# Turning attention probabilities: a product with diag(1/sum) against normalization on VectorE and a turn by the identity

## The reference

```
logits = einsum('bthd,btkhd->bthk', q, k_sel) * A_HEAD_DIM ** -0.5
logits = where(valid, logits, -inf)
p = softmax(logits, axis=-1)
return einsum('bthk,btkhd->bthd', p, v_sel)
```

## Time and profile before

| | |
|---|---|
| median of 3 runs | 1298.71 us (1297.08 to 1299.79) |
| profiled execution, its own time | 1302.94 us |
| its span, first to last instruction | 1301.3 us |
| TensorE busy (matmuls) | 1123.8 us, 86% |
| VectorE busy | 624.9 us, 48% |
| ScalarE busy | 321.8 us, 25% |
| mean granted TensorE clock | 0.93 |

### The profile page before, as it was taken

How to read it: one execution, slowest core, us unless ns; L and a number is a source line. 1 busy time by engine, 2 the same in 40 slices (tenths; PEclk the granted TensorE clock), 3 DMA queues, 4 the chain that set the end, 5 groups by cost and what they waited for, 6 DMA issues and landing times.

```text
span 1301.3 us, 24857 instructions
## 1 busy us (share of the span) xinstructions
PE 1123.8 (86%) x9930; PEld 682.8 (52%) x9930; DVE 624.9 (48%) x1363; ACT 321.8 (25%) x758; POOL 162.9 (13%) x225
## 2 busy tenths in 40 slices
PE   8999999997899279998599999999789973999930
PEld 3577778973545223332256777899454541333310
DVE  0056899867243511111643589988653443011128
ACT  0243341305321111111244343322242210211100
POOL 0140008005000110000301000350410002000030
PEclk9999999998899589999799999999989975999975
DMA  7199110008450869996522111100486057699742
GB/s 293 45 391 379 51 64 18 7 13 283 184 225 9 348 234 377 420 423 240 191 77 60 64 49 65 33 22 5 147 293 239 24 214 279 254 418 425 290 153 89
DMA packets 58357, 240.56 MB, mean 185 GB/s; under 512 B 8738, under 2 KB 20162, under 8 KB 48834
## 3 DMA queue, kind: packets, MB, share of 16 engines
q1 hardware_dynamic: 38608, 169.15, 33.8%
q0 software_dynamic: 14592, 52.10, 10.9%
q10 hardware_dynamic: 5042, 17.71, 3.4%
HBM read 190.38 MB, written 50.78 MB: 185 GB/s over the span
## 4 chain that ended last, share of the span: by engine, by line
PE 83%; DVE 6%; ACT 3%; issue 3%; DMA 2%; DVEq 2%; POOL 1%; POOLq 0%; ACTq 0%
PE ps L767 20%; PE ps L1360 13%; PE ps L936 11%; PE ps L1317 9%; PE ps L1375 7%; PE ps L747 4%; PE ps L713 4%; PE ps L1185 2%; PE ps L1347 2%; ACT arena L1452 1%; PE ps L827 1%; PE ps L723 1%; PE ps L1284 1%; PE ps L1296 1%; DVEq L2545 1%
## 5 line engine op out<-in xcount | busy, mean ns | idle before, releaser
L1452 ACT ACTIVATE arena<-ps 128x512 f32<-128x512 f32 (+11 forms) x336 | 140.3, 454 | 599.2 <-PE ps L767 148.3
L767 PE MATMUL ps<-arena 128*128 128x272 f32 x1088 | 259.7, 396 | 0.0
L767 PEld LDWEIGHTS ps<-arena 128*128 128x128 f32 x1088 | 204.9, 190 | 48.8 <-issue 4.9
L1360 PE MATMUL ps<-arena 128*32 128x512 f32 x1536 | 169.7, 592 | 4.8 <-ACT arena L1452 4.8
L936 PE MATMUL ps<-arena 64*64 64x64 f32 (+3 forms) x4016 | 145.2, 231 | 3.9 <-DVE arena L2248 2.5
L936 PEld LDWEIGHTS ps<-arena 64*64 64x64 f32 x4016 | 134.6, 134 | 15.0 <-issue 10.0
L1317 PE MATMUL ps<-arena 128*128 128x512 f32 x256 | 115.8, 609 | 0.0
L1360 PEld LDWEIGHTS ps<-arena 128*32 128x32 f32 x1536 | 51.3, 109 | 116.9 <-issue 116.9
L1375 PE MATMUL ps<-arena 128*32 128x512 f32 x768 | 87.4, 595 | 3.4 <-DVE arena L2713 2.0
L1317 PEld LDWEIGHTS ps<-arena 128*128 128x128 f32 x256 | 48.6, 194 | 58.9 <-issue 58.8
L2707 DVE COPY arena<-ps 128x256 f32<-128x256 f32 x24 | 10.2, 425 | 140.2 <-PE ps L1392 140.2
(11 more groups left out here) (351 smaller groups left out, 1287.8 us busy)
## 6 DMA issues: line engine op xcount, KB each, us to landing
arena<-in_w_gu SPq DMA_DIRECT2D x32, 2048.0 KB, 13.7
arena<-in_w_dn SPq DMA_DIRECT2D x32, 1024.0 KB, 14.4
arena<-in_wf SPq DMA_DIRECT2D x34, 512.0 KB, 3.7
rows_in<-arena POOLq DMA_DIRECT2D x12, 1024.0 KB, 25.8
arena<-rows_in SPq DMA_DIRECT2D x24, 512.0 KB, 13.7
rows_out<-arena ACTq DMA_DIRECT2D x24, 512.0 KB, 8.6
arena<-in_cache_v POOLq DMA_DIRECT2D x64, 128.0 KB, 5.6
arena<-in_cache_k SPq DMA_DIRECT2D x64, 128.0 KB, 6.8
```

The lines of the kernel that those rows point to most:

```text
L767: mm = pe.matmul(ps[:, 2 + 2 * h + n % 2, 0:HALF], m.wf[n % 3][:, c, :], m.xT[:, c, h * HALF:h * HALF + HALF], start=c == 0, stop=c == KC - 1)
L1360: mm = pe.matmul(ps[q, 3 + k, :], m.xgT[:, c, q], m.w_gu[HOME[i]][:, c, :], start=c == 0, stop=c == KC - 1, skip_group_check=True)
L1452: return act.activation(out, in_, ACT.Copy)
```

## The change

VectorE no longer multiplies the tile of probabilities. It multiplies the identity, for each of the four heads, with the reciprocal sums of the rows, which gives four diagonal 128x128 matrices (`m.weigh_p`, two buffers by turns). TensorE then multiplies each block of unnormalized exponentials with the head's diagonal matrix in an ordinary matmul, in place of the transpose with the identity. With the block as the stationary operand the result is the block turned, each column scaled by its query's reciprocal sum. VectorE waits before it writes a buffer: for tile 0 until the third gate event has come (the memory was `m.y2`), for tile 2 until the turns of tile 0 are done, for tile 3 until those of tile 1 are done. The wait of tile 1 is for a count already reached.

```diff
@@ memory
+    m.weigh_p = [view(R4 + 2880 + 2 * T + 512 * k, 4, P) for k in range(2)]
@@ tensor_program, output(i)
                 for c in range(i + 1):
-                    mm = pe.transpose(ps[:, 4 + h % 2, P * c:P * c + P], m.lg[i][:, h, P * c:P * c + P], ident)
+                    mm = pe.matmul(ps[:, 4 + h % 2, P * c:P * c + P], m.lg[i][:, h, P * c:P * c + P], m.weigh_p[i % 2][:, h, :],
+                                   start=True, stop=True)
                 mm.then_inc(s["pt_mm"], 1)
@@ vector_program, normed(i)
-            w = P * (i + 1)
-            x = m.lg[i]
             dve.wait_ge(s["p_exp"], nth(l, "p_exp", i + 1))
             dve.reciprocal(m.rsum[i], m.ssum[i])
             dve.drain()
-            tt(x, x, m.rsum[i].unsqueeze(2).broadcast_to([P, 4, w]), mul).then_inc(s["p_ready"], 1)
+            if i:
+                dve.wait_ge(s["pt_mm"], nth(l, "pt_mm", 4 * (i - 1)))
+            else:
+                dve.wait_ge(s["yn_mm"], nth(l, "yn_mm", 3))
+            tt(m.weigh_p[i % 2], ident.unsqueeze(1).broadcast_to([P, 4, P]), m.rsum[i].unsqueeze(2).broadcast_to([P, 4, P]), mul)\
+                .then_inc(s["p_ready"], 1)
```

## The result

The changed kernel takes 1302.47 us in the median of 20 runs, the kernel before 1298.49 in the median of 20: +4.0 us, ratio 1.0032 with a 95% interval of 1.0018 to 1.0046. The fastest run of each is 1300.58 and 1294.63 us, 6.0 apart. The forecast was 1303.1.

A forecast was written before the change was run, and what follows sets the result against it. TensorE was taken to bound the kernel, at 83% of the chain. VectorE 0, added passes 6.0 and half-clock passes 2.1, less 3.7 of returned clock, gave +4.4 us on 1298.71: 1303.1 us, range 1299.2 to 1307.8.

The forecast's parts named there:

- VectorE at 0: Attention: 6.4 us less VectorE time and its added waits both cost or gain 0, being off the chain.
- Two passes against one: Turns on TensorE: an f32 product takes two passes, a turn one, so 80 passes and 80 loads more.
- Rival 5: Turns on TensorE: such a product takes four passes, 18 us in all, 1317 us; chance 0.02.
- rival 3: Turns on TensorE: the product costs no second pass and the clock returns part, middle 1296.8 us; chance 0.07.
- Exposed or hidden: Four tiles' turns: added passes cost 0.11 us each where exposed, nothing where hidden; 3.0 us a layer, 6.0 in all.
- Rival 4: Turns on TensorE: loads stand in front of passes, 2 us a layer on top of the forecast, 1307; chance 0.05.
- The clock: TensorE in attention: half-clock passes add 2.1 us, filled idle time ahead of tile 3 gives back 3.7.
- +2.1 for passes at half: Tile 1 of layer 0 and tile 3 of both layers: added passes at half clock cost double, 2.1 us more.
- -3.7 returned: Tile 3, both layers: less idle time ahead keeps the clock up, giving back two thirds of 5.5 us.
- Rival 1: TensorE in attention: the clock falls where it fell before, +8.1 us, 1306.8; chance 0.20.
- Rival 2: TensorE in attention: full clock through tile 3 and layer 0's tiles 0 and 1, +1.1 us, 1299.8; chance 0.26.

The follow-up runs named there:

- experiment 9: Kernel before with TensorE's idle time filled and VectorE scaling the identity instead of normalizing, turns by the plain identity: 1293.17 us, ratio 0.9961 to the kernel before.
- experiment 1: Kernel before with each turn made an ordinary product with the plain identity, VectorE still normalizing: 1301.46 against 1297.18 us, ratio 1.0036.
- experiments 7 and 8: Kernel before with only heads 0 and 1 of every tile turned twice: ratio 0.9983; with only heads 2 and 3 turned twice: ratio 1.0046.
- experiment 4: Kernel before with only tile 3's first two heads turned twice, in TensorE's idle time: 1297.30 against 1297.18 us, ratio 0.9999.
- filled pair: Kernel before and changed kernel, each with filler work in TensorE's idle time throughout the attention stage: 1294.09 and 1300.29 us.
- 5: Kernel before with filler matmuls and repeated turns in every TensorE idle time of the attention stage: 1294.09 us, ratio 0.9967 to the kernel before.

## Why the prediction was right

**VectorE at 0: right.** The eight products came at 0.694 us, VectorE waited nowhere for a turn, and its half alone moved the time by nothing that can be told (experiment 9), with the other half alone making the whole loss (experiment 1).

**Two passes against one: right.** 160 records for 80, and 160 loads. A doubling of turns without any product reproduces 2.64 of the 3.2 us a layer. Tile 3's first eight blocks took 1.09 us as turns and 2.05 as products. Rival 5, four passes, is ruled out by this and by the 160 records, and rival 3, no second pass, by the same. The Trainium skill ("TensorE: Matmul & The Clock Gate", Terms) calls transpose mode 4x faster for FP32; these 2.05 and 1.09 us are about 2x, and the measurement decides.

**Exposed or hidden: right.** For tiles 0 and 1 together the prediction had 1.06 us, measured 1.13; for tile 2 0.96 and 1.09; for tile 3 0.98 and 1.00. The partly hidden first heads of tiles 1 and 2, two times 0.2, measured 0.22 and 0.23. In sum 6.0 against 6.4. The idle time left ahead of tile 3, 0.8 in the text and 0.9 by its own end of the turns at 333.7, came as 0.91. Rival 4 (loads ahead of passes, 2 us a layer more) falls: loads lie beside, and what the product costs above a doubled turn is 0.6 a layer, for which the prediction had 0.05 for each exposed group, 0.4 to 0.5 a layer.

**The clock: right in sign and place, too small in size, and weakly argued.** The prediction had +2.1 for passes at half and -3.7 returned, together -1.6; the runs give 4.0 - 6.2 = -2.2, with the wide interval said above. That filled idle time ahead of tile 3 keeps the clock there is shown by where the same passes stand (experiments 7 and 8). Over all profiles tile 3 was below 1.00 in 6 of the 8 layers where TensorE idles 1.87 us ahead of it, and in none of the 18 where that time is filled or the turns are doubled there. The prediction drew it from the recovery at 340 us in rows 8, but value passes stood among the turns there, so that row doesn't show that turns count; experiments 4 and 7, where turns alone were added, do.

What the prediction didn't see is that the kernel before isn't at one clock either. Its runs go from 1294.6 to 1307.8 us, and their mean granted clock goes along: 0.934 in the run of 1294.97 us, 0.924 in that of 1307.82. Also in the profiles code far from the attention takes some 2 us more or less with its clock. "The clock as before" was therefore no fixed thing to add 2.1 to or to take 3.7 from.

Rival 1, the clock as before, falls: tile 3 is at 1.00 in both layers, and its +8.1 lies outside the interval of 2.3 to 6.0 us. Rival 2 is, for the attention alone, what the two profiled executions show: all stretches at 1.00, and 0.8 us more from the column sums to the head values where it had +1.1. But that holds against one execution of before whose clock fell in the attention. Against runs at their best the loss is the whole price of the passes (the fastest of each are 6.0 apart), and in the median it is 4.0, outside rival 2's +1.1.

The sum of +4.4 against +4.0 is better than its parts, and that is luck: by the medians the price of the passes was 0.2 too low and what the clock returned 0.6 too low, the two errors partly cancel, and an interval of 2.3 to 6.0 can't tell forecasts apart to 0.4. The two thirds of the returned clock were a guess.

**Open.** Why filling only tile 3 (experiment 4) left the median where it was, while taking only that filler from the filled stage costs 4.6 us. In the profile of experiment 4 the attention is 2.5 us shorter than before (98.68 against 101.17 us), with its clock fall at another place. This fits a clock that falls somewhere as long as one hole is left, but one profile doesn't show that. It is also open whether the falls outside the attention depend on what is done inside it.

## What to carry to other kernels

Count records per source line before exchanging one TensorE operation for another: an f32 product here is two passes where a turn is one, and that alone decided this change. Ask where each added pass stands: behind a wait it is free and may hold the clock, between two busy groups it costs its full time. When two kernels differ by a few us and TensorE's clock falls at random, compare them with the idle time filled in both, and by the stretches that the change touches: here both layers then agreed to 0.01 us. The spans as a whole don't, since the clock still falls elsewhere (1291.4 and 1298.4 us for the filled pair, 7.0 apart, with 6.4 in the stretches).

## What the runs showed of the hardware

Redundant turns and products in TensorE's idle time made the kernel 4.6 and 4.7 us faster and its spread narrower (1292.75 to 1294.46 us over twelve runs against 1294.97 to 1304.21). The way from the column sums to the first values, where VectorE and ScalarE do most of the work, shrank too, from 21.2 to 19.85 us, as the logits between them ran at the full clock: in layer 0 those of tile 2 took 1.59 us of the chain instead of 2.90. The filler ahead of tile 3 consists of turns alone, and the clock held. The Trainium skill ("TensorE: Matmul & The Clock Gate", Part 4: PE-mode transpose) says that turns don't count as busy for the clock in the same way. Here the turns added in experiments 4, 5 and 7 kept tile 3 at 1.00 in all six layers, so the measurement differs from the page.
